# Gathering expert tokens by matmul from SBUF in place of a fetch from DRAM, with a ninth weight buffer

## What is computed

```python
def swiglu(x, wg, wu, wd):
    return (jax.nn.silu(x @ wg) * (x @ wu)) @ wd          # 1024 -> 3584 -> 1024 for an expert

def moe_swiglu(x, w_router, we_gate, we_up, we_down):     # x: 256 x 1024, float32
    logits = x @ w_router
    top_vals, top_idx = lax.top_k(logits, 2)
    gates = jax.nn.softmax(top_vals)
    combine = einsum("bske,bsk->bse", one_hot(top_idx, 8), gates)
    out = 0
    for e in range(8):
        out = out + combine[..., e:e + 1] * swiglu(x, we_gate[e], we_up[e], we_down[e])
    return out
```

## Time and profile before

| | |
|---|---|
| median of three runs | 1256.97 us |
| the profiled execution | 1257.12 us |
| its span, first to last instruction | 1255.4 us |
| PE busy | 1214.8 us, 97% |
| DVE busy | 720.1 us, 57% |
| ACT busy | 585.7 us, 47% |
| POOL busy | 39.9 us, 3% |
| moved by DMA | 434.43 MB |

### The profile page before, as it was taken

The page is one execution under the profiler, slowest core; times in us unless marked ns, Lnnn a source line. Parts: engine busy times, 40 slices in busy tenths (PEclk is TensorE's granted clock), DMA queues, the critical chain, the costliest instruction groups (busy, mean ns, idle before and its releaser), DMA issues.

```text
span 1255.4 us, 15006 instructions
## 1 busy us (share of the span) xinstructions
PE 1214.8 (97%) x6061; PEld 853.4 (68%) x6061; DVE 720.1 (57%) x649; ACT 585.7 (47%) x496; POOL 39.9 (3%) x60
## 2 busy tenths in 40 slices
PE   9999999999999999999999999999999999999994
PEld 8988888888988557656755665674575566567541
DVE  6978655568888455545635643654564365455524
ACT  5576444445767245334533533543452354345321
POOL 0100000002000000000000000000000000000010
PEclk9999999999999999999999999999999999999998
DMA  9957565546458899999999999999999999999995
GB/s 317 350 173 240 196 201 184 187 134 236 151 191 323 336 404 420 404 411 420 420 420 407 419 419 419 419 420 420 406 419 419 420 420 413 421 420 417 419 395 232
DMA packets 109678, 434.43 MB, mean 346 GB/s; under 512 B 8884, under 2 KB 50916, under 8 KB 96292
## 3 DMA queue, kind: packets, MB, share of 16 engines
q1 hardware_dynamic: 106016, 421.07, 85.3%
q0 software_dynamic: 3504, 12.32, 2.7%
q10 hardware_dynamic: 84, 0.02, 0.0%
HBM read 428.40 MB, written 4.98 MB: 345 GB/s over the span
## 4 chain that ended last, share of the span: by engine, by line
PE 86%; DVE 6%; DMA 3%; ACT 3%; issue 2%; SPq 0%; DVEq 0%; ACTq 0%
PE turn L2189 16%; PE turn L2153 15%; PE turn L2193 8%; PE accp L2129 6%; PE accp L2167 6%; PE turn L1857 4%; PE turn L1854 4%; PE accp L2172 4%; DVE w_lo L1111 4%; PE accp L1745 3%; PE accp L1746 3%; PE accp L1747 3%; DMA raw<-in_we_down 3%; PE turn L1856 2%; PE turn L1855 2%; ACT w_hi L773 2%
## 5 line engine op out<-in xcount | busy, mean ns | idle before, releaser
L1111 DVE TENSOR_TENSOR w_lo<-raw,w_hi 128x2048 fp32r<-128x2048 f32 (+3 forms) x202 | 425.5, 2120 | 212.4 <-ACT w_hi L773 210.3
L773 ACT CAST w_hi<-raw 128x2048 fp32r<-128x2048 f32 (+1 forms) x196 | 352.1, 1804 | 163.6 <-DMA raw<-in_we_down 49.9
L2153 PE MATMUL turn<-raw,x_few 128*64 128x448 f32 x784 | 161.6, 547 | 2.1 <-issue 1.2
L2189 PE MATMUL turn<-w_hi,a_hi 128*128 128x448 f32 x496 | 128.5, 378 | 2.6 <-ACT y_work L956 1.1
L2189 PEld LDWEIGHTS turn<-w_hi,a_hi 128*128 128x128 f32 x496 | 87.9, 188 | 51.9 <-issue 37.2
L2193 PE MATMUL turn<-w_lo,a_hi 128*128 128x448 f32 x496 | 121.4, 367 | 0.7 <-DVE w_lo L1111 0.7
L2167 PE MATMUL accp<-w_hi,t_both 128*128 128x512 f32 x448 | 117.6, 404 | 3.6 <-ACT w_hi L773 3.6
L2189 PE MATMUL turn<-w_hi,a_lo 128*128 128x448 f32 x496 | 120.7, 365 | 0.0
L2167 PEld LDWEIGHTS accp<-w_hi,t_both 128*128 128x128 f32 x448 | 79.8, 188 | 50.9 <-issue 36.4
L2153 PEld LDWEIGHTS turn<-raw,x_few 128*64 128x64 f32 x784 | 51.1, 136 | 83.3 <-issue 75.7
L2193 PEld LDWEIGHTS turn<-w_lo,a_hi 128*128 128x128 f32 x496 | 92.5, 188 | 10.0 <-DVE w_lo L1111 2.2
(11 more groups left out here) (283 smaller groups left out, 1454.9 us busy)
## 6 DMA issues: line engine op xcount, KB each, us to landing
raw<-in_we_gate SPq DMA_DIRECT2D x97, 896.0 KB, 10.9
raw<-in_we_up SPq DMA_DIRECT2D x97, 896.0 KB, 10.2
raw<-in_we_down SPq DMA_DIRECT2D x77, 1024.0 KB, 11.0
raw<-in_w_in SPq DMA_DIRECT2D x18, 1024.0 KB, 8.6
ln_rows<-in_we_gate SPq DMA_DIRECT2D x16, 896.0 KB, 10.2
raw_more<-in_we_up SPq DMA_DIRECT2D x16, 896.0 KB, 9.6
raw_more<-in_we_down SPq DMA_DIRECT2D x14, 1024.0 KB, 11.1
raw_more<-in_we_gate SPq DMA_DIRECT2D x15, 896.0 KB, 11.0
```

Source lines behind the costliest of these rows:

```text
L773: nc.scalar.copy(w_hi[:, part_of(p), 0:filled(p)], raw_of(p)).then_inc(hi_done, 1)
L1111: return nc.vector.tensor_tensor(out, whole, hi.bitcast(f32), ALU.subtract)
L2153: last = nc.tensor.matmul(half_banks[which][rows, c, :], x_few[:, e % 2, k, :], w[:, h, c, :], start=(k == 0), stop=(k == KD - 1))
L2189: nc.tensor.matmul(wide_banks[:, c, :], left, wh[:, c, :], start=(k == 0 and left is x_hi_k), stop=False)
```

## The change

PE gathers the tokens itself at each visit: for each of the eight column blocks of x it multiplies the block of x in SBUF, as the stationary operand, by `pick`, over both tiles of 128 tokens, as plain float32. The steps that found the numbers of the tokens and the fetch by POOL are gone; the copy of x to `token_rows` stays. `choose` writes one expert's `pick` at a time, in two places by turns, behind the visit that read the place. x must stay unscaled until the last visit, so that `scale_tokens` goes to unit 13, both tiles at once; the transposition of the last `pick` goes to unit 10. In unit 0 the visit stands behind five gate pieces. The space that is left holds a ninth raw buffer, `raw_rows`, of which `more_rows` is a part; the last 16 pieces still use seven. SP reads an expert's number when it comes to its first gate piece, one at a time.

```diff
-    SUM_AT = (0, 1, 2, 3)
-    PICK_AT = 4
+    PICK_AT = 10
+    SCALE_AT = 13
...
         if i == 0:
-            return "ggggggSgg" + "uuuuuuVuu"
+            return "gggggVggg" + "uuuuuuuu"
...
-        order = ("gTgTdggdggSdggd" if light(i - 1) else "gTgTgTdgTggSdggd") + "uudVuudWuuduud"
+        order = ("gTgTdggdggKdggd" if light(i - 1) else "gTgTgTdgTggdggd") + "uudVuudWuuduud"
...
-    MOE_SLOTS = [(MOE_AT + j) % RING for j in range(RING)] + [RING, RING + 1]
-    LAST_TURNS = MOE_PIECES // len(MOE_SLOTS) * len(MOE_SLOTS) - 2 * len(MOE_SLOTS)
+    LN_SLOT, ROWS_SLOT = RING + 1, RING + 2
+    MOE_SLOTS = [(MOE_AT + j) % RING for j in range(RING)] + [RING, LN_SLOT, ROWS_SLOT]
+    LAST_TURNS = (MOE_PIECES - 2 * RING) // len(MOE_SLOTS) * len(MOE_SLOTS)
...
-        return MOE_SLOTS[(j - LAST_TURNS) % (len(MOE_SLOTS) - 1)]
+        return MOE_SLOTS[(j - LAST_TURNS) % MOE_SLOTS.index(LN_SLOT)]
...
+                elif SLOTS[p] == ROWS_SLOT:
+                    sp.wait_ge(row_squares, NT * 3)
...
-                if (which, i, pair) == ("gate", ORDER.index("L"), 0):
+                kind = ORDER[i]
+                if (which, s, pair) == ("gate", 0, 0) and (kind, k) != ("H", 0):
                     sp.wait_ge(experts_known, 1)
-                    ranked_expert = [sp.value_load(expert_of[0:1, q:q + 1], min_val=1, max_val=E - 1)
-                                     for q in range(OTHERS)]
+                    q = rank(kind, k)
+                    ranked_expert[q] = sp.value_load(expert_of[0:1, q:q + 1], min_val=1, max_val=E - 1)
...
-            def fetch_tokens(f):
-                pool.wait_ge(tokens_known, f // 2 + 1)
-                if f == 0:
-                    pool.wait_ge(tokens_written, 16 * NT)
-                else:
-                    pool.wait_ge(xg_turned, visit_chunks(visits_before(f)))
-                count = FEW if FETCHED[f][0] == "L" else P
-                nc.gpsimd.indirect_dma_start(more_rows[0:count, :], None, token_rows, bass.IndirectOffsetOnAxis(
-                    ap=token_of[0:count, f:f + 1], axis=0)).then_inc(tokens_loaded, 16)
...
             for j in range(ALL_ROWS):
+                if j == 1:
+                    pool.wait_ge(piece_used, upto(ROWS_SLOT_LEFT))
...
             def scale_tokens(n):
                 act.wait_ge(x_lo_ready, NT + 1)
+                act.wait_ge(xg_turned, visit_chunks(len(VISITS)))
...
-                            if i in (1, 2):
-                                scale_tokens(i - 1)
+                            if i == SCALE_AT:
+                                for n in range(NT):
+                                    scale_tokens(n)
...
+            def choose_next(j):
+
+                if j + 2 < OTHERS:
+                    dve.wait_ge(xg_turned, visit_chunks(j + 1))
+                    choose(j + 2)
...
                     elif c in "VW":
                         rest_of_tokens(visit_at(i), "VW".index(c))
+                        if c == "W" or "W" not in order_in(i):
+                            choose_next(visit_at(i))
...
-            def turn_tokens(j, c):
+            def gather_tokens(j, c):
                 i, f = VISITS[j]
                 if c:
                     pe.wait_ge(xg_done, visit_chunks(j) + 1)
                 else:
-                    pe.wait_ge(tokens_loaded, 16 * (f + 1))
+                    pe.wait_ge(pick_ready, NT + f + 1)
                     if i:
                         turn_left(i - 1)
...
                 count, part = (FEW, range(KD)) if FETCHED[f][0] == "L" else (P, range(4 * c, 4 * c + 4))
                 for at, k in enumerate(part):
-                    last = nc.tensor.transpose(tokens_bank[:, at * count:(at + 1) * count],
-                                               more_rows[0:count, k * P:(k + 1) * P], ident[0:count, 0:count])
+                    for n in range(NT):
+                        last = nc.tensor.matmul(tokens_bank[:, at * count:(at + 1) * count],
+                                                x[:, n, k * P:(k + 1) * P],
+                                                pick[:, n, f % 2, 0:count].bitcast(f32), start=(n == 0), stop=(n == NT - 1))
                 last.then_inc(xg_turned, 1)
```

More of the change, by code:

```diff
@@ L147, in order_in @@
         if i == 0:
-            return "ggggggSgg" + "uuuuuuVuu"
+            return "gggggVggg" + "uuuuuuuu"
         if i == N_UNITS - 1:
             return "gTgTgTdgTdgdgdgdgdd" + "uuuuuuuu"
-        order = ("gTgTdggdggSdggd" if light(i - 1) else "gTgTgTdgTggSdggd") + "uudVuudWuuduud"
-        if i not in SUM_AT:
-            order = order.replace("S", "K" if i == PICK_AT else "")
+        order = ("gTgTdggdggKdggd" if light(i - 1) else "gTgTgTdgTggdggd") + "uudVuudWuuduud"
+        if i != PICK_AT:
+            order = order.replace("K", "")
         if visit_at(i) is None:
@@ L232, in hybrid_trunk_kernel @@
         FILLS.append(so_far[slot])
-    LN_SLOT_LEFT = last_in[RING + 1]
+    LN_SLOT_LEFT, ROWS_SLOT_LEFT = last_in[LN_SLOT], last_in[ROWS_SLOT]
     ctx = ExitStack()
@@ L286, in hybrid_trunk_kernel @@
         ys_rows = sb("ys_rows", [P, D])
-        more_rows = sb("more_rows", [P, D])
+        with ExitStack() as beyond:
+            over_hT_parts = beyond.enter_context(nc.sbuf_tensor("over_hT_parts", [P, 2, COL], f32r))
+        raw_rows = sb("raw_rows", [P, PIECE])
         raw_more = sb("raw_more", [P, PIECE])
-        over_hT_parts = sb("over_hT_parts", [P, 2, COL], f32r)
+        more_rows = raw_rows[:, 0:D]
         slot_rows = nc.dram_tensor("slot_rows", [HEAVIES * P + (LIGHTS - 1) * FEW, D], f32, kind="Internal").ap()
@@ L317, in hybrid_trunk_kernel @@
         before_whole, ones_whole = work[:, 3088:3216], work[:, 3216:3344]
-        ids_whole = work[:, 3344:3344 + 2 * NT].rearrange("p (n i) -> p n i", n=NT)
         centred = y_work[:, :].rearrange("p (n d) -> p n d", n=NT)
@@ L401, in hybrid_trunk_kernel @@
         hT_bank = accp[:, 3, :]
-        sums_bank = accp[:, 3, 0:4]
         tokens_bank = accp[:, 3, :]
@@ L446, in hybrid_trunk_kernel @@
             sem(n) for n in ("gathered", "xg_hi_ready", "xg_lo_ready", "xg_turned", "xg_rounded", "xg_done"))
-        tokens_written, tokens_summed, tokens_known, tokens_loaded = (
-            sem(n) for n in ("tokens_written", "tokens_summed", "tokens_known", "tokens_loaded"))
+        tokens_written = sem("tokens_written")
         slots_written, slots_read = sem("slots_written"), sem("slots_read")
@@ L485, in raw_of @@
                 return raw[:, slot, 0:filled(p)]
-            whole = raw_more[:] if slot == RING else ln_rows[:, :, :].rearrange("p j d -> p (j d)")
-            return whole[:, 0:filled(p)]
+            if slot == LN_SLOT:
+                return ln_rows[:, :, :].rearrange("p j d -> p (j d)")[:, 0:filled(p)]
+            return (raw_rows if slot == ROWS_SLOT else raw_more)[:, 0:filled(p)]
         def landed(p):
@@ L502, in hybrid_trunk_kernel @@
         ALL_ROWS = len(ROWS)
-        rows_in = [ys_rows[:], more_rows[:], a_hi[:, 0:D].bitcast(f32), a_lo[:, 0:D].bitcast(f32)]
+        rows_in = [ys_rows[:], more_rows, a_hi[:, 0:D].bitcast(f32), a_lo[:, 0:D].bitcast(f32)]
         def over_piece(e, j):
@@ L523, in rows_written @@
             return 16 * sum(2 if kind == "L" else 1 for kind, _ in KEPT[:j])
-        token_rows_in = [ys_rows[:], more_rows[:]]
+        token_rows_in = [ys_rows[:], more_rows]
         SCATTER = [(n, half) for n in range(NT) for half in range(2)]
@@ L734, in _ @@
                     write_rows(kept_in(i - 1))
[L735 to L738, removed]
             write_rows(kept_in(N_UNITS - 1))
@@ L1211, in finish_tile, with choose @@
                                                in1=ln_rows[:, 1, :], op0=ALU.mult, op1=ALU.add).then_inc(ln_norm, 2)
[L1213 to L1223, removed]
+            def choose(f):
+                ek, c = FETCHED[f], f % 2
+                for n in range(NT):
+                    if ek == LAST_ONE:
+                        to = pick[:, n, c, :].rearrange("p (i t) -> p i t", i=2)
+                        places = slot_iota[:, 0:FEW].unsqueeze(1).to_broadcast([P, 2, FEW])
+                    else:
+                        to, places = pick[:, n, c, :], slot_iota[:, 0:P]
+                    last = nc.vector.tensor_scalar(to, places, slot_at[:, n, rank(*ek):rank(*ek) + 1], None,
+                                                   ALU.is_equal)
                 last.then_inc(pick_ready, 1)
+            def choose_next(j):
+                if j + 2 < OTHERS:
+                    dve.wait_ge(xg_turned, visit_chunks(j + 1))
+                    choose(j + 2)
             step(nc.vector.memset(mean_conv[:].bitcast(f32), 0.0))
@@ L1448, in rank_experts @@
                 choose(0)
+                choose(1)
                 step(nc.vector.tensor_tensor(below, at_rank, slot_iota[:, 1:E].unsqueeze(1).to_broadcast(
@@ L2341, in _ @@
                         turned += 1
[L2342 to L2345, removed]
```

(5 more changed lines are left out.)

20 lines of the change are left out of this document (2 added, 18 removed).

## The result

The changed kernel takes 1273.67 us (median of four runs, 1273.29 to 1273.87) against 1257.01 us before (median of four): a ratio of 1.0129, 95% interval 1.0114 to 1.0144. It is 16.7 us slower; the forecast was 18.8 us over the median. The profiled execution took 1273.87 us with a span of 1271.8 us, 16.4 us longer than before.

The account below looks back on a forecast made before the run. PE was taken to bound the kernel, with DMA close behind. The profiled 1257.12 us + 18.9 (gather 27.3 less 8.4 removed) - 0.1 (ninth buffer) gave 1275.9 us, 1275.8 on the median's scale; range 1268 to 1282 us.

Parts of the forecast that it names:

- What bounds: Expert units: PE sets the pace with DMA close behind, since lengths of two-unit stretches follow PE's work at equal bytes.
- The price of the gather: PE at seven visits: 224 plain float32 instructions at 0.122 us, +27.3 us, bounds 26.6 to 32.0 us.
- What goes: PE loses transposes of fetched rows (3.6 and 2.8 us) and sums of token numbers (2.0 us), together 8.4 us.
- The tail: Last 16 pieces, seven buffers in both kernels: the end keeps its distance from the last heavy down piece, 0.
- The ninth buffer: One more piece in flight or landed: removes one 1.5 us landing wait, then DVE's order is late, -0.1 us.
- the reads: SP reads expert numbers one at a time, where it waits for buffers: 0, or 2 us if that cover were gone.
- the moved steps: Scaling of x in unit 13 and `choose` with DVE's new wait lie hidden: 0, else 1 us once for scaling.
- DMA as the pace: Rival at each piece's landing: DMA sets the pace, 6.2 + 2.2 us less, 1248.7 us; chance 0.03.
- the stall behind the gather: Rival at the down piece behind each visit: PE waits 2.28 us for `w_lo`, seven times, 1291.9 us; chance 0.05.
- The soaked-up idle time: Rival in the expert units: earlier landings make PE's 14.5 us of waits vanish, 1261.4 us; chance 0.05.
- One instruction for a matmul: Rival in the gather: 112 instructions at 0.119 us, 13.3 us, net +4.9, 1262 us; chance 0.03 including the skill's rule.
- the 81 ns: Skill's matmul spacing applied to the 112 gathers: 9.1 us, 0.7 us more than what goes, 1257.8 us.

Follow-up runs that it names:

- The third experiment: Kernel before with one fetch of token rows in place of seven, PE's work unchanged: 1257.93 us, ratio 1.0003.

## Why the prediction was right

**What bounds.** Right. PE's work set the pace: more or less of the gather moves the time one for one, less DMA does not move it. That DMA is close behind was right too, and closer than it looked: an edit worth 9.5 us of PE's idle time, under 1% of the whole, was enough to meet it in the kernel before. The argument from the lengths of the stretches was weaker than it was put. By length and rate in the earlier trace rows the seventh stretch, the shortest, also moved the least but for the first (44.4 MB, the others 44.5 to 45.1). Only the first separates the two, as the longest, with the most work and the fewest bytes (43.5 MB). The third experiment settles it.

**The price of the gather.** 27.3 us forecast, 26.4 measured. That half the columns save nothing was right. The pace of 0.122 us was too high, because of how it was taken: busy time divided by count. In an unbroken run of matmuls each counts in this quotient with the distance to the next, but the last with its whole 0.27 us, so that short runs look slower. Both rows that the forecast used, L2044 and L1967, are two runs of 16 in the trace. A heavy visit is also two runs of 16, but a light one is a single run of 32. One run of L2044 from the kernel before, then a heavy and a light one from the changed kernel:

```profile
363.06 1.89 PE L2044 MATMUL accp<-wr,work 128*128 128x64 f32 x16
...
671.57 1.95 PE L2240 MATMUL accp<-pick,x 128*128 128x128 f32 x16
781.29 3.68 PE L2240 MATMUL accp<-pick,x 128*128 128x64 f32 x32
```

What one more instruction costs is read from the doubled gather: 29.0 - 14.7 us for 128 of them at 64 columns and 22.4 - 11.7 us for 96 at 128 columns, 0.112 us both times. So the term was too large by 0.9 us, all of it in the light visits. The upper bound, from L2253, was too high for the same reason: those are runs of two and four.

**What goes.** 8.4 us forecast by busy time. The first stretch, which lost two sums, grew by 1.06 us where 2.7 - 1.15 = 1.55 was due. PE's idle part in it fell from 2.50 to 2.09 us, which the forecast left out: two waits of 0.2 us, for `w_hi` and `w_lo`, are no longer there. Why they went is open. In the fourth and sixth stretches the light visits grew by 2.87 and 2.79 us, where the measured price gives 3.68 - 0.7 = 2.98. PE's idle part did not change there (2.27 and 2.27 us, 2.29 and 2.26 us), so the last 0.1 to 0.2 us is open too.

**The tail.** 0 forecast, -0.65 us measured. The issues keep their distance, as the forecast had it. The remainder comes from landings that PE waits for at the end. In the 15 us behind the last heavy down piece DMA moves 334 GB/s, before 370, and five down pieces land 13.6 us after their issue (median), before 15.0; that this is the cause is argued, not shown. The clock is no rival: before, PE's granted clock was 0.58 from 1231.3 to 1234.5 us, behind a wait of 2.7 us, and 8 matmuls took 3.18 us where they now take 1.94, but PE then waited for two more landings, 0.6 and 1.8 us.

Together, of the 2.4 us by which the span grew less than forecast: 0.9 us is the gather's pace, 0.65 the tail, 0.4 the idle time that went in the first stretch, and some 0.45 is spread over the light visits and open. By place, the span grew by 2.5 us up to the first stretch, by 14.6 us in the seven, and by -0.65 us behind them.

**The ninth buffer, the reads, the moved steps.** 0 each for the reads and the moved steps, -0.1 us for the buffer. Neither the buffer nor the reads made a difference that can be measured. That the new wait of DVE and the scaling of x cost nothing shows in PE's waits: from 470 to 1210 us none is new, and the seventh stretch, in which x is scaled, grew by 0.08 us.

**The rivals.** DMA as the pace and the stall behind the gather fell as argued; for the stall, PE's longest wait from 470 to 1210 us is the 1.4 us of DVE's order, where it was put at 2.28 us. The soaked-up idle time fell for the reason given: the wait came from DVE's order and stayed, and one edit of this order took it away. One instruction for a matmul fell by count, and so did the 81 ns of the Trainium skill's page "TensorE: Matmul & The Clock Gate", section "Back-to-back issue gap". The runs add what separates the two: float32r passes as one instruction, 0.11 to 0.12 us a matmul, plain float32 as two, 0.22 to 0.24 us. Neither is near 81 ns.

**What the change misses.** It buys 6.2 us of DMA time with 16.7 us of PE time in a kernel bound by PE. The fetch that it replaces was issued a visit ahead and cost PE a short transpose. Of the versions that compute the right result, the best one tried is the kernel before with DVE's earlier split, 1254.78 us. It beats both.

## What to carry to other kernels

Where two engines both show 97% or more, cut the run into stretches with nearly the same bytes and different work, see which the length follows, and then change the load of one engine alone; a share of 1.0 on DMA did not mean that relief of DMA was worth anything. A gather by a one-hot matmul is priced in instructions, so look up a matmul of the same type in the trace, in runs of about the same length, and count the instructions against the code. Small idle times of the bounding engine are worth following to the instruction behind which their releaser stood: here an order on DVE was worth 11 us in one kernel, but 2.5 us in the other, where DMA came next.

## What was not expected of the hardware

- DMA's busy share fell from 1.02 to 1.00 when its rate fell from 416 to 405 GB/s in the third stretch; within the changed kernel 393 and 420 GB/s show as 0.99 and 1.01. No two-unit stretch that was looked at held more than 420 GB/s, in the kernel before, the changed one, or the three experiments with an earlier split.
- A run of 32 instructions of plain float32 matmuls takes as long at 32 columns as at 64 (128 instructions in four runs: 14.6 and 14.7 us), and one more instruction costs 0.112 us at 64 columns and at 128. In this range the columns are nearly free, and two light experts gathered in one matmul would cost little more than one. This was not tried.
